# Head units of the first mixer as 512-column products, one product for all bias rows, index logits as two 64-row tiles

## The reference

```
h = rms_norm(x, norm_mix_g[l]);  proj = h @ w_in[l]
q, k, v, xr, gr, sc_b, sc_c, sc_x, g_pre = split(proj)
# attention of a head; a query sees only earlier keys of the 256
s = (q * d_head**-0.5) @ k.T + rel_table[t5_bucket(dist)];  s = where(dist >= 0, s, -inf)
y_a = softmax(s) @ v
# the second block's index score, which picks 256 // 4 keys for each query
s = einsum("bqhd,bsd->bqhs", qi, k_idx) * IDX_HEAD_DIM ** -0.5     # 16 heads of 64
score = einsum("bqhs,bqh->bqs", relu(s), wi)
```

## Time and profile before

| | us |
|---|---|
| median of 3 runs (2730.95 to 2732.28) | 2731.0 |
| the profiled execution | 2730.99 |
| its span | 2729.1 |
| PE busy | 2708.7 (99%) |
| PE weight loads busy (beside PE) | 2358.0 (86%) |
| DVE busy | 1668.3 (61%) |
| ACT busy | 1280.0 (47%) |
| DMA, mean rate | 187 GB/s |

### The profile page before, as it was taken

The page is one execution under the profiler, slowest core; times in us unless marked ns, Lnnn a source line. Parts: engine busy times, 40 slices in busy tenths (PEclk is TensorE's granted clock), DMA queues, the critical chain, the costliest instruction groups (busy, mean ns, idle before and its releaser), DMA issues.

```text
span 2729.1 us, 42542 instructions
## 1 busy us (share of the span) xinstructions
PE 2708.7 (99%) x15136; PEld 2358.0 (86%) x15136; DVE 1668.3 (61%) x2329; ACT 1280.0 (47%) x1721; POOL 22.8 (1%) x51
## 2 busy tenths in 40 slices
PE   7999999999999999999999999999999999999999
PEld 6999998888888888888888889999888888888887
DVE  5466766555555655655656566777776565565554
ACT  5454555444444543544434454455554344454443
POOL 0100000000000000000000000000000000000000
PEclk9999999999999999999999999999999999999999
DMA  7655555666666555555555555544455555556555
GB/s 260 207 167 180 175 178 183 203 201 195 204 197 200 182 188 193 185 193 188 189 193 185 189 180 168 173 148 155 155 178 185 193 189 189 193 185 193 188 190 170
DMA packets 140038, 509.01 MB, mean 187 GB/s; under 512 B 15911, under 2 KB 16167, under 8 KB 139656
## 3 DMA queue, kind: packets, MB, share of 16 engines
q1 hardware_dynamic: 136024, 494.37, 55.8%
q0 software_dynamic: 2736, 10.75, 1.2%
q10 hardware_dynamic: 1152, 2.10, 0.2%
HBM read 502.96 MB, written 4.19 MB: 186 GB/s over the span
## 4 chain that ended last, share of the span: by engine, by line
PE 97%; DVE 1%; DMA 1%; ACT 1%; issue 0%; SPq 0%; ACTq 0%; DVEq 0%
PE acc L1697 18%; PE acc L1698 9%; PE pS L1732 4%; PE acc L1732 4%; PE pS L1734 4%; PE pT L1734 4%; PE pT L1732 4%; PE pS L1733 4%; PE pT L1733 4%; PE acc L1734 4%; PE acc L1733 4%; PE acc L1682 4%; PE acc L1684 4%; PE acc L1683 4%; PE acc L1714 3%; PE acc L1716 3%
## 5 line engine op out<-in xcount | busy, mean ns | idle before, releaser
L995 DVE TENSOR_TENSOR wlo<-raw,whi 128x1024 fp32r<-128x1024 f32 x938 | 1147.4, 1224 | 849.8 <-ACT whi L538 847.7
L538 ACT ACTIVATE whi<-raw 128x1024 fp32r<-128x1024 f32 x938 | 992.2, 1059 | 1032.8 <-PE pT L1734 345.4
L1697 PE MATMUL acc<-a_w,whi 128*128 128x512 f32 x2048 | 724.6, 399 | 0.1
L1698 PE MATMUL acc<-a_w,wlo 128*128 128x256 f32 x2048 | 575.1, 281 | 0.0
L1697 PEld LDWEIGHTS acc<-a_w,whi 128*128 128x128 f32 x2048 | 384.8, 188 | 96.8 <-DVE a_w L1025 0.8
L1698 PEld LDWEIGHTS acc<-a_w,wlo 128*128 128x128 f32 x2048 | 386.9, 189 | 0.3
L1682 PE MATMUL acc<-a_w,whi 128*128 128x256 f32 x896 | 257.6, 287 | 0.0
L1683 PE MATMUL acc<-a_w,whi 128*128 128x256 f32 x896 | 253.5, 283 | 0.0
L1684 PE MATMUL acc<-a_w,wlo 128*128 128x256 f32 x896 | 253.5, 283 | 0.0
L1682 PEld LDWEIGHTS acc<-a_w,whi 128*128 128x128 f32 x896 | 171.8, 192 | 3.4 <-issue 3.0
L1714 PE MATMUL acc<-a_w,whi 128*128 128x256 f32 x592 | 173.9, 294 | 0.0
(11 more groups left out here) (403 smaller groups left out, 4216.8 us busy)
## 6 DMA issues: line engine op xcount, KB each, us to landing
raw<-stream SPq DMA_DIRECT2D x938, 512.0 KB, 3.4
gbias<-gateb POOLq DMA_DIRECT2D x12, 256.0 KB, 3.7
xF<-x SPq DMA_DIRECT2D x4, 512.0 KB, 7.7
X<-x_rows POOLq DMA_DIRECT2D x1, 2048.0 KB, 10.5
bias_scratch<-brow POOLq DMA_DIRECT2D x8, 256.0 KB, 3.5
out<-X ACTq DMA_DIRECT2D x8, 256.0 KB, 4.6
bias<-bias_scratch POOLq DMA_DIRECT2D x8, 128.0 KB, 3.7
wg<-gates POOLq DMA_DIRECT2D x8, 128.0 KB, 3.5
```

The costliest lines, as they stand in the source:

```text
L538: A(whi[:, slot, :], raw[:, slot, :], ACT.Copy).then_inc(s.hi_done, 1)
L995: TT(wlo[:, slot, :], raw[:, slot, :], whi[:, slot, :].bitcast(F32), SUB).then_inc(s.lo_done, 1)
L1697: MM(ps, wh, wide[:, k0 + k, :], start=start and k == 0, stop=False, skip_group_check=True)
L1698: last = MM(ps[:, 0:T], wl, wide[:, k0 + k, 0:T], start=False, stop=not start and k == KC - 1, skip_group_check=True)
```

## The change

There are three edits, and a DMA that comes with the second.

1. The head units use `chunk_wide`. The two halves of the bank must be added, so each of the 56 units has a new copy on ACT (`half`, L670 of the changed kernel) before `prep(c+1)` and behind the side work, and on DVE an addition (L1003) and the multiplication (L1005) in place of the one multiplication.
2. The bias rows of all eight heads come from one matmul with the table's eight columns: 8 partitions by 512. ACT copies 8 rows once. The write to scratch is one DMA, which reads each of the 8 partitions 128 times.
3. The index logits of the two heads are separate matmuls on rows 0 to 63 and 64 to 127, 128 and then 256 columns each, into pT and pS. The ReLUs read 384 columns of each.

The diff, cut to its core:

```diff
-            for h in range(HEADS):
-                pool.wait_ge(s.bias_copied, h + 1)
-                pool.dma_start(bias_scratch[h, 0:P * 512].rearrange("(p c) -> p c", p=P),
-                               brow[:, h, :]).then_inc(bias_out[h % 2], 16)
-            for k in range(2):
-                pool.wait_ge(bias_out[k], 16 * HEADS // 2)
+            pool.wait_ge(s.bias_copied, 1)
+            pool.dma_start(bias_scratch.rearrange("h (p c) -> h p c", p=P),
+                           brow[0:HEADS, :].unsqueeze(1).to_broadcast([HEADS, P, 512])).then_inc(s.bias_out, 16)
+            pool.wait_ge(s.bias_out, 16)
...
                 for j in range(L1_UNITS):
                     c = At(16 + 2 * L1_UNITS * i + 2 * j)
-                    if i == 0 and 1 <= j <= 4:
-                        bias_rows(j - 1)
                     prep(c)
+                    if i == 0 and j == 1:
+                        act.wait_ge(s.bias_ps, 1)
+                        A(brow[0:HEADS, :], pO[0:HEADS, :], ACT.Copy).then_inc(s.bias_copied, 1)
                     if i:
                         side1(j, At(i - 1))
+                    a = L1_UNITS * i + j
+                    act.wait_ge(s.mm_done, c.value(2))
+                    if a >= 2:
+                        act.wait_ge(s.l1_summed, a - 1)
+                    apart(act)
+                    A(half[:, a % 2, :], acc[a % 2][:, T:2 * T], ACT.Copy).then_inc(s.l1_copied, 1)
                     prep(c.plus(1))
...
-                A(irelu[:, 0:T], pT[:, 0:T], ACT.Relu)
-                A(irelu[:, T:3 * T], pS[:, 0:2 * T], ACT.Relu).then_inc(s.idx_relu, 1)
+                A(irelu[:, 0:384], pT[:, 0:384], ACT.Relu)
+                A(irelu[:, 384:768], pS[:, 0:384], ACT.Relu).then_inc(s.idx_relu, 1)
...
-            def evac(c, a, dst, scale=rB, rows=slice(0, P)):
-                acc_wait(c)
-                TT(dst, acc[a.mod(2)][rows, 0:T], scale[rows], MUL).then_inc(s.evacuated, 1)
+            def evac(a, dst):
+                dve.wait_ge(s.l1_copied, a.value(1))
+                if a.least() > 0:
+                    dve.wait_ge(s.evacuated, a.value())
+                TT(t2, acc[a.mod(2)][:, 0:T], half[:, a.mod(2), :], ADD).then_inc(s.l1_summed, 1)
+                dve.wait_ge(s.l1_summed, a.value(1))
+                TT(dst, t2, rB, MUL).then_inc(s.evacuated, 1)
...
-                    chunk(c, a, a_w, 0, stop=False)
-                    chunk(c.plus(1), a, a_w, 8, start=False)
+                    chunk_wide(c, a, a_w, 0)
+                    chunk_wide(c.plus(1), a, a_w, 8, start=False)
                     if i == 0 and j == 0:
                         pe.wait_ge(s.oh_landed, 16)
                         pe.wait_ge(s.tab_landed, 16)
-                    if i == 0 and j < 4:
-                        bias_rows(j)
+                        MM(pO[0:HEADS, :], tab[0:33, 0:HEADS], oh[0:33, :], start=True, stop=True).then_inc(s.bias_ps, 1)
...
-                MM(pT[:, 0:T].rearrange("p (h k) -> p h k", h=2), q[:, 0:128],
-                   kibd.rearrange("p (h k) -> p h k", h=2)[:, :, 0:128], start=True, stop=True)
-                MM(pS[:, 0:2 * T], q[:, 128:256], kibd, start=True, stop=True).then_inc(s.idx_pe, 1)
+                rows = [slice(64 * e, 64 * e + 64) for e in range(2)]
+                for e, ps in enumerate((pT, pS)):
+                    r = rows[e]
+                    MM(ps[:, 0:128], qib[r, n % 3, 0:128], kibd[r, T * e:T * e + 128], start=True, stop=True)
+                for e, ps in enumerate((pT, pS)):
+                    r = rows[e]
+                    last = MM(ps[:, 128:384], qib[r, n % 3, 128:256], kibd[r, T * e:T * e + T], start=True, stop=True)
+                last.then_inc(s.idx_pe, 1)
```

More of the change, by code:

```diff
@@ L174, in __init__ @@
         self.up_copied = make("up_copied")
+        self.l1_copied = make("l1_copied")
+        self.l1_summed = make("l1_summed")
         self.setup_act = make("setup_act")
@@ L180, in __init__ @@
         self.bias_copied = make("bias_copied")
+        self.bias_out = make("bias_out")
         self.causal_landed = make("causal_landed")
@@ L314, in program @@
         rn = rn_f.rearrange("p (k t) -> p k t", t=T)
-        sqacc = sb("sqacc", 2 * T)[0].rearrange("p (k t) -> p k t", t=T)
+        half = sb("half", 2 * T)[0].rearrange("p (k t) -> p k t", t=T)
         sq = sb("sq", 2 * T)[0].rearrange("p (k t) -> p k t", t=T)
@@ L379, in program @@
         tab = take("tab", 8)
-        brow = take("brow", HEADS * 512).rearrange("p (k c) -> p k c", k=HEADS)
+        brow = take("brow", 512)
         xF = take("xF", DT * T).rearrange("p (m t) -> p m t", t=T)
@@ L423, in program @@
         gb_landed = [ctx.enter_context(nc.semaphore(f"gb_landed{k}")) for k in range(2)]
-        bias_out = [ctx.enter_context(nc.semaphore(f"bias_out{k}")) for k in range(2)]
         def pcol(name, k=0):
@@ L653, in _ @@
                 prep(At(c))
[L655 to L659, removed]
             for i in range(8):
@@ L995, in prep @@
                 TT(wlo[:, slot, :], raw[:, slot, :], whi[:, slot, :].bitcast(F32), SUB).then_inc(s.lo_done, 1)
-            def acc_wait(c):
-                dve.wait_ge(s.mm_done, c.value(1))
-            def evac(c, a, dst, scale=rB, rows=slice(0, P)):
-                acc_wait(c)
-                TT(dst, acc[a.mod(2)][rows, 0:T], scale[rows], MUL).then_inc(s.evacuated, 1)
+            def evac(a, dst):
[5 more added lines that the diff above has]
+                TT(dst, t2, rB, MUL).then_inc(s.evacuated, 1)
             def norm_lo(m, gain):
@@ L1198, in _ @@
                         side1(j, At(i - 1), (i + 1) % 2)
-                    last = c.plus(1)
                     if j < 4:
-                        evac(last, a, (b.q, b.k, b.xr[:, 3:3 + T], b.gr)[j])
+                        evac(a, (b.q, b.k, b.xr[:, 3:3 + T], b.gr)[j])
                     elif j == 4:
-                        evac(last, a, l1_c)
+                        evac(a, l1_c)
                     elif j == 5:
-                        evac(last, a, t1)
+                        evac(a, t1)
                         dve.wait_ge(s.evacuated, a.value(1))
@@ L1208, in _ @@
                     else:
-                        evac(last, a, b.b)
+                        evac(a, b.b)
                     prep(c.plus(1))
@@ L1364, in idx_add @@
                         dve.wait_ge(s.idx_dve, 4 * n + 2)
-                    STT(score[:, 0:128], irelu[:, 128 * e:128 * e + 128], wi_tok[:, 0, 2 * n + e:2 * n + e + 1],
+                    STT(score[:, 0:128], irelu[:, 384 * e:384 * e + 128], wi_tok[:, 0, 2 * n + e:2 * n + e + 1],
                         score[:, 0:128], MUL, ADD).then_inc(s.idx_dve, 1)
-                    STT(score[:, 128:384], irelu[:, T + T * e:2 * T + T * e], wi_tok[:, 1, 2 * n + e:2 * n + e + 1],
+                    STT(score[:, 128:384], irelu[:, 384 * e + 128:384 * e + 384], wi_tok[:, 1, 2 * n + e:2 * n + e + 1],
                         score[:, 128:384], MUL, ADD).then_inc(s.idx_dve, 1)
@@ L1671, in _, with chunk_wide @@
             MM = nc.tensor.matmul
-            def chunk(c, a, wide, k0, start=True, stop=True):
+            def chunk_wide(c, a, wide, k0, start=True, late=None):
                 slot, ps = c.mod(NSLOT), acc[a.mod(2)]
@@ L1677, in chunk @@
                 if start and a.least() >= 2:
[L1678 to L1691, removed]
                     pe.wait_ge(s.evacuated, a.value(-1))
@@ L1799, in side1 @@
                     attn_pv(t, v[:, 0, :], v[:, 1, :])
[L1802 to L1807, removed]
             def spread(r, ready):
@@ L1835, in _ @@
                         pe.wait_ge(s.tab_landed, 16)
-                    if i == 0 and j < 4:
-                        bias_rows(j)
+                        MM(pO[0:HEADS, :], tab[0:33, 0:HEADS], oh[0:33, :], start=True, stop=True).then_inc(s.bias_ps, 1)
                     if i == 0 and j == 6:
-                        pe.wait_ge(s.bias_copied, 8)
+                        pe.wait_ge(s.bias_copied, 1)
                     if i:
@@ L1945, in idx @@
                     pe.wait_ge(s.idx_relu, n)
-                q = qib[:, n % 3, :]
-                MM(pT[:, 0:T].rearrange("p (h k) -> p h k", h=2), q[:, 0:128],
-                   kibd.rearrange("p (h k) -> p h k", h=2)[:, :, 0:128], start=True, stop=True)
-                MM(pS[:, 0:2 * T], q[:, 128:256], kibd, start=True, stop=True).then_inc(s.idx_pe, 1)
+                rows = [slice(64 * e, 64 * e + 64) for e in range(2)]
[6 more added lines that the diff above has]
+                last.then_inc(s.idx_pe, 1)
             def q_stat(p):
```

## The result

The changed kernel takes 2742.64 us (median of 6 runs, 2740.9 to 2745.31), the kernel before 2730.94 beside it. The ratio is 1.0041, with a 95% interval of 1.0031 to 1.0051: 11 us slower, outside the range of 2721 to 2738. The profiled execution took 2745.31 with a span of 2743.6, so it is compared with the span of 2729.1: 14.5 us more.

A forecast was written before the change was run, and what follows sets the result against it. It took TensorE to bound the kernel, 97% of the chain that ended last. 9.3 us saved less 8.2 lost to the late bias left 1.1 off 2731.0: forecast 2730 us, own range 2726 to 2735, with rivals 2721 to 2738.

The forecast's parts named there:

- What bounds the kernel: Whole kernel: TensorE is 97% of the chain that ended last, so fewer columns there win time unless TensorE then waits.
- 512 columns: Head units: a k-step in two matmuls takes 0.3532 us instead of 0.36, saving 6.1 us over 56 units.
- the copy's chain: ACT's added copy and DVE's addition: 4.4 us lost at six heads, 0.05 at the first, 1.95 at the gates.
- Bias product: Bias rows behind head units: one product costs 1.13 us where four pairs cost 8.36, so 7.2 us saved.
- Index logits: 64-row tiles run beside each other: a set costs 1.00 us instead of 1.30, saving 2.4 us for eight.
- the 9.3 us saved: Whole change: 7.2 from bias rows plus 2.4 from index logits less 0.3 from the wide head units.
- The write's landing: Bias write to HBM from 8 partitions: issued at 71.3 us, takes 42 us, landed at 113.3.
- This is what decides: Bias path through HBM: the bias comes 8.4 us late, and TensorE waits 8.2 us more at the first head's transposes.
- rival (b): During the bias write: it starves the weight stream, TensorE stands 12.5 to 19.5 us, 2738 us in all; chance 17%.
- The lateness step: First head: a late bias holds DVE's later work and is paid at the transposes, 8.2 us.

The follow-up runs named there:

- the kernel with the spread write: The changed kernel with the same 2 MB bias write read from 128 partitions, 8 copies from each, instead of 8 partitions: 2723.77 us, ratio 0.9968 to the kernel before.
- Lateness alone: The changed kernel with its bias write from 128 partitions and the eight bias reads held back until TensorE has done 34 chunks: 2733.67 us, ratio 1.0006.

## Why the prediction was wrong

**What bounds the kernel, 512 columns, the copy's chain: right.** In the units a k-step is 0.347 to 0.353. Waits at the middle transposes are 1.0 each instead of 0.3, at the gates 3.0 where 2.9 was said; net nothing, as the -0.3 said (edit 1 alone: 1.0001).

**Bias product: right.** It costs 0.95 (67.57 to 68.52) and 0.1 at the next step, where 1.13 was forecast.

```profile
67.57 1.02 PE L1815 MATMUL pO<-oh,tab 33*8 33x512 f32 x2
68.52 0.50 PE L1684 MATMUL acc<-a_w,whi 128*128 128x512 f32 x1
```

**Index logits: right.** Read as the earlier trace rows were, from the last plain matmul ahead of the set (1681.78) to the second behind it (1683.07), less two steps of 0.12, a set costs 1.05, with 1.00 forecast and 1.30 before. The four matmuls of the two heads start in pairs, within 0.01 us. Edit 3 alone gave 0.9990.

```profile
1681.78 0.28 PE L1703 MATMUL acc<-a_w,wlo 128*128 128x256 f32 x1
1681.99 0.37 PE L1927 MATMUL pT<-kibd,qib 64*128 64x128 f32 x1
1682.00 0.37 PE L1927 MATMUL pS<-kibd,qib 64*128 64x128 f32 x1
...
1683.07 0.28 PE L1702 MATMUL acc<-a_w,whi 128*128 128x256 f32 x1
```

So the 9.3 us saved were there: the kernel with the spread write has them, with 8.7 (0.32%).

**The write's landing: near in size, by luck.** It took 46.7 against 42. The 42 were the geometric middle of two bounds, 10.5 and 168, with no row that spoke for either more than for the other.

**The failed step: "This is what decides" priced that write by its own lateness only, 8.2 us, and left the stream unharmed.** The stream was harmed, as rival (b) had it, at 17%. In the place of one wait at the first transposes the runs show chunks at less than half their pace for 46 us. The bias then wasn't waited for: its reads were out at 124.8, and DVE came to it at 135.74, without any idle time before it.

```profile
135.74 0.29 DVE L1092 SCALAR_TENSOR_TENSOR L<-pS,bias 128x128 f32<-128x128 f32 x1
```

The argument against (b), that X and the stream shared the engines and the chunks still came, compared sizes alone: X goes to 128 partitions, the write comes from 8.

**Rival (b) was too small.** It gave 12.5 to 19.5 us of stands and 2738; the stands are 14.0. What it lacked is the clock: 5.3 us of slow steps. The outermost dimension of 8, which the prediction held to speak for (b), is not the cause by itself: the writes from 8 partitions 16 and 4 apart have it and cost nothing. The edits' 9.3 and the 19.3 give 2731 - 9.3 + 19.3 = 2741, close to the 2742.64.

**The lateness step had the wrong path too.** A bias 8.1 us late is paid at the gates' product, whose weights are loaded behind it, and not at the transposes. It cost 11.2, some 4 either way, where 8.2 was said: 8.0 of wait and at least 1.8 of slow work, a term that the step had left out. Lateness alone made 1.0006, a tie with the kernel before; it isn't the cause of the 1.0041. That the two late effects don't add in the changed kernel is argued from its trace, in which the reads land before they are needed.

## What to carry to other kernels

A broadcast that a DMA reads many times from few partitions is to be priced by what else must pass the same partitions' way, not by when its own data are needed: here each chunk of a stream that fills 128 partitions came at less than half its pace while 8 neighbouring ones were read. Put the source on partitions that spread out, by more result rows, which cost TensorE 0.1 us here (1.06 us from start to start instead of 0.95). And a stand of TensorE is to be priced with the slow steps that follow it, here 5.3 us on top of 14.0.

## What the runs showed of the hardware

The DMA queues during the changed kernel's write, 74 to 120 us (packets, MB, share of the engines' time), and what landed:

```profile
q0 software_dynamic: 1040, 2.10, 40.4%
q1 hardware_dynamic: 986, 3.61, 23.8%
...
raw<-stream SPq DMA_DIRECT2D x8, 512.0 KB, 20.6
```

The engines' time is taken to 64% by packets while they move some 125 GB/s; the kernel before has 62% at its 199 GB/s. So they were held rather than loaded, as far as these shares tell. By the port rule of the Trainium skill (SBUF — State Buffer, Door 1: The DMA port swizzle) half of the write, 1.05 MB, and a sixteenth of the stream's 3.61 MB, 0.23, pass one port: 1.28 MB in 46.7 us is 27 GB/s, an estimate that agrees with the page's 27.2. It would mean that a port's rate is shared by what is read from SBUF and what is written to it. The write from 8 partitions 16 apart points the same way: with four ports, a quarter of 2.10 MB and a sixteenth of the stream's 3.56 pass each in 26.2 us, 28.5 GB/s by the same estimate, a little above the page's figure. By the write alone the two would be 22.5 and 20.0, further apart. No run here moves one direction without the other, so the sharing is inferred, not shown. From 4 apart and from all 128 the same sum gives 24 and 20 GB/s; there something else bounds.

The Trainium skill (DMA: Bandwidth & Descriptors, Rules for kernel authors) has an outermost dimension of 8 confined to 8 DMA engines. The writes from 8 partitions 16 and 4 apart have that dimension too, and cost nothing. They did take longer than the 10.1 us from 128, so this rule may have a share in that; by itself it makes no loss.
